# First block's attention: scores in pieces of at most 512 keys, one piece ahead, and reciprocal sums spread through memory

## The reference, cut to what matters

```python
for window, dilation in DILATED_PATTERNS:
    o_i, lse_i = dilated_window_attn(q, k, v, window, dilation)
    outs.append(o_i); lses.append(lse_i)
mix_w = jax.nn.softmax(jnp.stack(lses, axis=0), axis=0)
o = jnp.sum(mix_w[..., None] * jnp.stack(outs, axis=0), axis=0)
attn_out = o.reshape(B, S, ATTN_WIDTH) * jax.nn.silu(g_attn)
```

## Time and profile before

| | |
|---|---|
| time, median of 3 runs | 2654.49 us (2652.89 to 2657.09) |
| the profiled execution | 2656.93 us |
| its span in the trace | 2655.1 us |
| mean granted TensorE clock in it | 0.979 |
| TensorE busy over the span | 2502.4 us, 94% |
| VectorE, ScalarE, GpSimd busy | 1255.3, 1142.3, 596.3 us |

### The profile page before, as it was taken

One profiled execution on the slowest core, in us unless ns is written; L12 is line 12 of the kernel. 1 busy time (PEld: TensorE's weight loads), 2 busy tenths in 40 slices (PEclk: granted clock), 3 DMA queues, 4 the chain that ended last, 5 costly groups with the idle time before them and its releaser, 6 DMA issues. The chain is left out here.

```text
span 2655.1 us, 30070 instructions
## 1 busy us (share of the span) xinstructions
PE 2502.4 (94%) x11958; PEld 2004.0 (75%) x11958; DVE 1255.3 (47%) x1583; ACT 1142.3 (43%) x1612; POOL 596.3 (22%) x497
## 2 busy tenths in 40 slices
PE   8999998889999999999999999998978999999992
PEld 6888874448787888878887877885866888888882
DVE  6420315554303112126443943014138888888886
ACT  4212225553341222124232732244225777777773
POOL 1312302213131222233121741254101111111100
PEclk9999999999999999999999999999988999999996
DMA  4313121203310031233225633351546999999995
GB/s 174 107 64 92 54 82 40 80 13 132 111 64 32 32 130 46 72 108 105 90 68 203 238 135 111 103 183 45 177 174 242 376 380 377 388 381 373 374 363 232
DMA packets 146581, 434.78 MB, mean 164 GB/s; under 512 B 16232, under 2 KB 66632, under 8 KB 133768
## 3 DMA queue, kind: packets, MB, share of 16 engines
q1 hardware_dynamic: 95536, 374.23, 37.5%
q10 hardware_dynamic: 38120, 31.50, 3.6%
q0 software_dynamic: 12784, 27.11, 2.9%
HBM read 377.70 MB, written 72.91 MB: 170 GB/s over the span
## 5 line engine op out<-in xcount | busy, mean ns | idle before, releaser
L2795 DVE TENSOR_TENSOR ex_w_lo<-ex_w,ex_w_hi 128x2048 fp32r<-128x2048 f32 x198 | 448.0, 2290 | 73.3 <-ACT ex_w_hi L2734 71.4
L2734 ACT ACTIVATE ex_w_hi<-ex_w 128x2048 fp32r<-128x2048 f32 x198 | 378.9, 1915 | 21.6 <-PE ex_pb L2665 14.5
L220 POOL TENSOR_TENSOR p_w_lo<-w_raw,p_w_hi 128x512 fp32r<-128x512 f32 (+1 forms) x146 | 191.3, 1343 | 624.7 <-ACT p_w_hi L248 593.2
L220 POOL TENSOR_TENSOR p_w_lo_rest<-w_raw,p_w_hi_rest 128x512 fp32r<-128x512 f32 x88 | 118.0, 1373 | 255.9 <-ACT p_w_hi_rest L248 255.9
L845 DVE CUSTOM_DVE_ANT_0 att_sc<-att_ps_s,logc 128x128 f32<-128x128 f32 (+7 forms) x96 | 71.7, 752 | 120.8 <-PE att_ps_s L780 120.4
L273 PE MATMUL p_ps<-p_w_hi,hT_hi 128*128 128x512 f32 (+1 forms) x320 | 120.7, 377 | 0.0
L275 PE MATMUL p_ps<-p_w_hi,hT_lo 128*128 128x512 f32 (+1 forms) x320 | 118.3, 370 | 0.0
L274 PE MATMUL p_ps<-p_w_lo,hT_hi 128*128 128x512 f32 (+1 forms) x320 | 118.0, 369 | 0.0
L248 ACT ACTIVATE p_w_hi<-w_raw 128x512 fp32r<-128x512 f32 (+1 forms) x133 | 74.6, 599 | 91.2 <-PE mix_ps_rest L275 49.3
L2434 POOL DMA_INDIRECT ex_x<-xn_rows,slot_token x33 | 34.2, 1036 | 346.4 <-PE ex_px L2639 323.9
L273 PE MATMUL ex_py<-ex_w_hi,ex_hT_hi 128*128 128x512 f32 x264 | 107.3, 407 | 1.9 <-DVE ex_hT_lo L2804 1.9
(11 more groups left out here) (507 smaller groups left out, 6260.4 us busy)
## 6 DMA issues: line engine op xcount, KB each, us to landing
ex_w<-w SPq DMA_DIRECT2D x99, 2048.0 KB, 13.8
w_raw<-w_in SPq DMA_DIRECT2D x42, 1024.0 KB, 5.1
w_raw<-w_out SPq DMA_DIRECT2D x8, 1024.0 KB, 8.0
x_rows<-o_x SPq DMA_DIRECT2D x16, 512.0 KB, 2.6
qk_columns<-ml_qk_first ACTq DMA_DIRECT2D x16, 512.0 KB, 3.2
w_raw<-w_xkv SPq DMA_DIRECT2D x8, 1024.0 KB, 6.2
plain_cols<-x SPq DMA_DIRECT2D x8, 512.0 KB, 8.3
w_raw<-w_in SPq DMA_DIRECT2D x16, 256.0 KB, 3.9
```

The source lines that it names most:

```text
L220: emit(self.lo(n)[:, 0:w], self.half(n // (KC // 2), w)[:, n % (KC // 2), :], self.hi(n)[:, 0:w].bitcast(F32), ALU.subtract).then_inc(self ...
L2734: nc.scalar.activation(w_hi[:, n % RING, :], raw_half(n), ACT.Copy).then_inc(hi_done, 1)
L2795: nc.vector.tensor_tensor(w_lo[:, n % RING, :], raw_half(n), w_hi[:, n % RING, :].bitcast(F32), ALU.subtract).then_inc(down_lo if m == "w2 ...
```

## The change

**Pieces.** A row of more than 512 keys becomes two pieces, of 512 and of the rest: 12 pieces a pair. Each piece takes one bank of each head, alternating by its number. `scores` waits until the piece two before it has been taken out by both heads' `maxes`. For the second piece of a row, `maxes` starts from the first piece's result, a column in `nmx_first`, and not from a number.

**One piece ahead.** `items()` yields pieces for rows. TensorE issues piece 0 first and then, at the place of piece n, piece n+1. VectorE and ScalarE stay at the places of the pieces and rows. With two pieces ahead of one block, VectorE does the first piece's second head and the second piece's first head before the block's copy.

**Sums.** `spread_sums` and its matmuls, `keep_scales` and TensorE's wait on it are gone. SP waits for the reciprocals, stores the 1024 floats of a half to `sums_dram` with one DMA, waits for that, and loads them with two DMAs, each repeating 512 floats over 64 partitions, into `scales`. Queries, keys, V and weights are loaded from the same queue between these steps, in a new order. GpSimd's `scale` for a half now stands at the half's block 3, and `gate` after block 3 of the next half (block 2 before).

The diff, with the loads' and waits' lines:

```diff
-def attention(c, heads, q_dram, k_dram, v_dram, mixT, next_weights):
+def attention(c, heads, q_dram, k_dram, v_dram, sums_dram, mixT, next_weights):
...
+    def pieces(i):
+        hp, a = divmod(i, NT)
+        first = PER * hp + (a if a < HALF else 2 * a - HALF)
+        return range(first, first + (1 if a < HALF else 2))
+    row_of_piece = {m: (i, m - pieces(i)[0]) for i in range(PAIRS * NT) for m in pieces(i)}
     def items():
...
-            yield "rows", a
+            yield "piece", a
...
-                if hp == 0:
-                    yield "rows", HALF + j
-                elif j == 0:
-                    yield "rows", NT * hp + NT - 1
+                if hp == 0 or j == 0:
+                    for m in pieces(HALF + j if hp == 0 else NT * hp + NT - 1):
+                        yield "piece", m
...
-            yield "sums", 2 * hp
...
-                    yield "rows", NT * (hp + 1) + (j if j < HALF else j - 1)
+                    for m in pieces(NT * (hp + 1) + (j if j < HALF else j - 1)):
+                        yield "piece", m
...
-                if j == HALF - 1:
-                    yield "sums", 2 * hp + 1
...
+        nmx_first = s.enter_context(nc.sbuf_tensor("att_negmax_first", [P, PAIRS * 2 * NT], F32))
...
-        ps_s = s.enter_context(nc.psum_tensor("att_ps_s", [P, 2, S], F32))
+        ps_s = s.enter_context(nc.psum_tensor("att_ps_s", [P, 2, 2, BANK], F32))
...
-        inverted, spread, scales_kept, scaled = (c.sem(f"att_{n}") for n in ("inverted", "spread", "scales_kept", "scaled"))
+        inverted, sums_out, scaled = (c.sem(f"att_{n}") for n in ("inverted", "sums_out", "scaled"))
+        sums_in = [c.sem(f"att_sums_in{b}") for b in range(2)]
...
-        def bank_of(i, k):
-            a = i % NT
-            at = BANK * (a % 2) if a < HALF else 0
-            return ps_s[:, k, at:at + (a + 1) * P]
+        def columns_of_piece(m):
+            i, part = row_of_piece[m]
+            return slice(BANK * part, min(BANK * part + BANK, (i % NT + 1) * P))
...
         def sum_column(i, k):
...
-            return NT * (2 * hp + a // HALF) + 2 * (a % HALF) + k
+            return NT * (2 * hp + a // HALF) + HALF * k + a % HALF
...
         def columns(d):
...
             @block.sync
             def _(sp):
-                for hp in range(1, PAIRS):
-                    if hp >= 2:
-                        sp.wait_ge(scored, NT * (hp - 1))
-                    heads.load_qk(sp, hp, q_dram, k_dram)
-                    if hp >= 2:
-                        sp.wait_ge(summed, PER * (hp - 1))
-                    heads.load_v(sp, hp, v_dram)
-                    if hp == 1:
-                        next_weights.load(sp, 0, 2)
-                    if hp == 3:
-                        next_weights.load(sp, 2, 3)
-                    if hp == 4:
-                        next_weights.load(sp, 3, 4)
+                def spread_sums(d):
+                    sp.wait_ge(inverted, d + 1)
+                    with nc.allow_non_contiguous_dma(reason="8 sums a partition"):
+                        sp.dma_start(sums_dram[d].rearrange("(r p o) -> p r o", p=P, o=1),
+                                     rden[:, NT * d:NT * (d + 1)].unsqueeze(2)).then_inc(sums_out, 16)
+                    sp.wait_ge(sums_out, 16 * (d + 1))
+                    if d >= 2:
+                        sp.wait_ge(scaled, d - 1)
+                    for k in range(2):
+                        sp.dma_start(scales[HD * k:HD * (k + 1), d % 2, :], sums_dram[d, BANK * k:BANK * (k + 1)].partition_broadcast(HD)
+                                     ).then_inc(sums_in[d % 2], 16)
+                heads.load_qk(sp, 1, q_dram, k_dram)
+                heads.load_v(sp, 1, v_dram)
+                next_weights.load(sp, 0, 2)
+                for hp in range(PAIRS):
+                    if 1 <= hp < PAIRS - 1:
+                        sp.wait_ge(scored, PER * hp)
+                        heads.load_qk(sp, hp + 1, q_dram, k_dram)
+                    spread_sums(2 * hp)
+                    if 1 <= hp < PAIRS - 1:
+                        sp.wait_ge(summed, PER * hp)
+                        heads.load_v(sp, hp + 1, v_dram)
+                    spread_sums(2 * hp + 1)
+                    if hp in (2, 3):
+                        next_weights.load(sp, hp, hp + 1)
...
             @block.gpsimd
             def _(pool):
                 def scale(d):
-                    pool.wait_ge(scales_kept, d + 1)
+                    pool.wait_ge(sums_in[d % 2], 32 * (d // 2 + 1))
...
-                    if kind == "sums":
-                        scale(n)
+                    if kind == "block" and block_at(n)[2] == 3:
+                        scale(2 * (n // PER) + block_at(n)[1])
...
             @block.tensor
             def _(pe):
-                def scores(i):
+                def scores(m):
+                    i, part = row_of_piece[m]
...
-                    if i >= 1:
-                        pe.wait_ge(maxed, 2 * i if a == 0 or a >= HALF else 2 * (i - 1))
-                    for u in range(0, (a + 1) * P, BANK):
-                        for k in range(2):
-                            at, end = slice(HD * k, HD * k + HD), min(u + BANK, (a + 1) * P)
-                            ins = pe.matmul(bank_of(i, k)[:, u:end], qk[hp % 2][at, 0, a * P:(a + 1) * P],
-                                            qk[hp % 2][at, 1, u:end], start=True, stop=True)
+                    if m >= 2:
+                        pe.wait_ge(maxed, 2 * (m - 1))
+                    to = columns_of_piece(m)
+                    for k in range(2):
+                        at = slice(HD * k, HD * k + HD)
+                        ins = pe.matmul(ps_s[:, k, m % 2, 0:to.stop - to.start], qk[hp % 2][at, 0, a * P:(a + 1) * P],
+                                        qk[hp % 2][at, 1, to], start=True, stop=True)
...
                 def turn(n, k):
...
-                def spread_sums(d):
-                    pe.wait_ge(inverted, d + 1)
-                    if d >= 1:
-                        pe.wait_ge(gated, d)
-                    for r in range(HALF):
-                        for k in range(2):
-                            at = NT * d + 2 * r + k
-                            ins = pe.matmul(ps_o[HD * k:HD * (k + 1), 1 - d % 2, r * P:(r + 1) * P],
-                                            rden[:, at:at + 1].to_broadcast([P, HD]), c.const("ident"),
-                                            start=True, stop=True)
-                    ins.then_inc(spread, 1)
                 def values(n):
...
-                    if j == 0 and n >= 1:
-                        pe.wait_ge(scales_kept, 2 * hp + half)
-                        if n > HALF:
-                            pe.wait_ge(gated, 2 * hp + half - 1)
+                    if j == 0 and hp >= 1:
+                        pe.wait_ge(gated, 2 * hp + half - 1)
...
+                scores(0)
...
-                    if kind == "rows":
-                        scores(n)
-                    elif kind == "sums":
-                        spread_sums(n)
+                    if kind == "piece":
+                        if n + 1 < len(row_of_piece):
+                            scores(n + 1)
...
             def _(dve):
...
-                def maxes(i, k):
+                def maxes(m, k):
+                    i, part = row_of_piece[m]
...
-                    dve.wait_ge(scored, i + 1)
+                    at, to = 2 * i + k, columns_of_piece(m)
+                    dve.wait_ge(scored, m + 1)
...
-                    nc.vector.tensor_tensor_reduce(row_of(i, k), bank_of(i, k), logc[:, S - (a + 1) * P:S], -SCALE, -NEG,
-                                                   ALU.add, ALU.min, nmx[:, 2 * i + k:2 * i + k + 1]).then_inc(maxed, 1)
+                    largest = nmx if m == pieces(i)[-1] else nmx_first
+                    so_far = nmx_first[:, at:at + 1] if part else -NEG
+                    if part:
+                        dve.wait_ge(maxed, 2 * m + k - 1)
+                    table = slice(S - (a + 1) * P + to.start, S - (a + 1) * P + to.stop)
+                    nc.vector.tensor_tensor_reduce(row_of(i, k)[:, to], ps_s[:, k, m % 2, 0:to.stop - to.start],
+                                                   logc[:, table], -SCALE, so_far, ALU.add, ALU.min,
+                                                   largest[:, at:at + 1]).then_inc(maxed, 1)
...
                 def invert(d):
...
-                    if kind == "rows":
+                    if kind == "piece":
...
-                        if late is not None and late < rows_before(n):
+                        if late is not None and row_of_piece[late][0] < rows_before(n):
...
-                        if j == 2 and n > 2:
+                        if j == HALF - 1 and n >= HALF:
...
             def _(act):
                 def exps(i):
...
-                        act.wait_ge(maxed, 2 * i + k + 1)
+                        act.wait_ge(maxed, 2 * pieces(i)[-1] + k + 1)
```

(18 more changed lines are left out.)

## The result

The changed kernel takes 2667.55 us in the median, against 2654.49 before. One of its five executions took 9897.54 us for a reason that no run explains; the median of the other four is 2667.2, and the ratio goes by them: 1.0044, with a 95% interval of 1.0032 to 1.0057. The profiled execution took 2666.88 us with a span of 2665.1, 10.0 more than before. So it lasts 218.7 us in place of 209.7: the stage holds 9.0 of the 10.0.

A forecast was written before the change was run, and what follows sets the result against it. TensorE was taken to set the pace, with waits in its holes. Terms 1.3 + 4 x 0.55 + 1.0 + 0.9 = 5.4 us off 2654.5 gave 2649.1; own range 2643 to 2655, 8 in 10 from 2637 to 2660.

The forecast's parts named there:

- the late memory path: Slower rival: store and loads exceed 14.7 us, gates hold VectorE's copies back, 10 us in all at the upper bound: 2659; chance 0.13.
- Sums through memory: Reciprocals' store and two loads: bounds 7.1 to 16.7 us, taken as 5.2 + 3 = 8.2.
- The queue: SP's order behind a store: next queries and keys go out near block 6, first asked for 19 us later.
- The loads: Two 128 KB loads repeating the reciprocals over 64 partitions: taken as 3 us of the 8.2 us path.
- The cover: Time from a first half's reciprocals to the gate, less GpSimd's work: 14.7 us steady, 9.9 in the last pair.
- The walk of the order: One steady pair on TensorE: five new waits for maxima, together 4.13 us; period 34.00 becomes 33.45, 0.55 us gained.
- The fast rival: Scores never wait for the second head's maximum: period 29.3 us, time 2628; chance 0.17.
- The second piece's bound from a column: VectorE's maxima of second pieces: no extra cost, or 0.08 us each, thrice a pair, 1.2 us in all.
- The sums: Twelve groups of 16 reciprocal matmuls leave TensorE: 0.87 us each, 1.74 a pair.
- The last pair: Period into the last pair, without scores of a next one: 32.57 us, 1.01 less than before.
- The first pair: Stage start to block 4's transposes: walked as 20.9 us against 23.4 before; 1.3 gained with low clock, 2.5 without.
- the dip: Low granted clock (0.72 before) on TensorE in the first pair, expected again, costing 1.2 us.

The follow-up runs named there:

- the turned store: Changed kernel, with VectorE transposing the reciprocals in 32x32 squares so a store writes 32 pieces of 128 bytes in four DMAs: 2651.53 us.
- Keys before the odd store: Changed kernel, with SP loading the next pair's queries and keys ahead of the second half's store: 2661.60 us.
- without the store: Changed kernel with the reciprocals' store and its wait left out, 512 floats of another input loaded instead (wrong numbers): stage 204.4 us, one execution of 2651.40.
- whole rows: Kernel before, its rows not cut into pieces, with the sums through memory and the store as 32 pieces of 128 bytes: 2647.57 us.
- pieces and maxima first: Changed kernel with VectorE's second-head maximum ahead of the next block's copy: 2650.27 us with sums on TensorE, 2641.55 through memory with 128-byte store pieces.
- the maxima first: Changed kernel with the store in 128-byte pieces, and VectorE doing the second head's maximum ahead of the next block's copy: 2641.55 us.

## Why the prediction was wrong

It forecast 2649 us, faster or the same; the kernel is slower, and the rival that came true is the late memory path, at 0.13, by more than the 10 us that it was given.

**The step that failed is the term "Sums through memory".** It priced the store at 5.2 us, after a load of 2048 single floats, and set aside the 11.0 us of a load of 1024 because larger loads were queued ahead of it. The store measured 9.9 us in the median, 8.4 to 12.0, and 8.4 us with nothing large ahead of it (575.56). The price lay by the upper bound and not by the lower one. The Trainium skill's rule that was quoted there (DMA: Bandwidth & Descriptors, Rules for kernel authors: one descriptor per element, rearrange) pointed to this side; the turned store, 2.2 us and a ninth of the small packets, agrees with it.

**Three links behind the price were not walked, or walked wrongly.**
- The queue. The step let the keys go out near block 6. There, at 448.03, 6.7 us after block 4's transposes, SP issued only the odd store, since it had served the even half first; the keys followed at 458.96, 17.6 after block 4, and at 528.68, 19.3 after it, with the weights ahead. That left 6.7 us before they were asked for in place of 19. Price: 0.7 + 3.35 us, and 1.2 of low clock. "Keys before the odd store" shows it.
- The loads. They took 5.6 to 5.8 us and not 3 for most first halves, and 10.9 where the next store followed them by 1.1 us. In the last pair store and loads came to 19.3 us (575.56 to 594.85) against a cover of 9.9: the excess of 9.4 is the gate's wait of 9.54. The cover was right and the path more than twice the 8.2 us that it was priced at, and above the upper bound of 16.7.
- The clock. No step charged a stall for what follows it. It was 1.2 us behind the keys and 1.4 behind the gate.

Together: 4.07 + 1.2 + 7.9 (9.37 less 1.44 at block 9) + 1.4 = 14.6 us, against 14.3 between the stages with and without the store. The rival had 2.0 us of lateness a pair for the steady gates; they did not wait at all (the only such wait in the stage is the 9.54), as 14.1 us from store to multiplication (504.18 to 518.24; 13.9 to 14.3 in the pairs before the last) just fits in 14.7. It had nothing for the keys.

**What held.** *The walk of the order:* 33.61 against 33.45 a pair; waits of 0.55, 0.82, 1.14, 0.70 and 0.31 idle against 0.63, 0.89, 1.38, 0.69 and 0.54, in the five places named; from start to start no step of the pair is off by more than 0.13. The fast rival without these waits did not come. *The second piece's bound from a column:* 746 ns against 683 for the plain 512, so 0.06 us each, within the 0 to 0.08. *The sums:* 1.74 to 1.76 us a pair in three comparisons (35.37 less 33.61, 33.34 less 31.59, 34.00 less 32.26), walked as 1.74. *The last pair:* 32.66 against 32.57. *The first pair:* 21.09 us against 20.9 without the dip; I had expected the dip and 22.1, because the walk had TensorE no busier there. It is busier, 13.31 us and not 10.99 between 385 and 402, and the dip is absent. That term was 1.0 us too small, and makes up for the 0.16 by which each of four periods is longer; that the stage without a store comes to 204.4 against 204.3 is in part this luck.

**Where the change stands without the store's fault.** The four versions with a cheap memory path or none divide its gain. Sums off TensorE gain 8.7 us by time at whole rows (2656.25 less 2647.57) and 8.7 with pieces and maxima first. The pieces in their order, one ahead and with the second maximum behind the copy, lose 4 (2651.53 less 2647.57). With the maxima first they gain 6 (2647.57 less 2641.55). So the pieces are worth something only together with VectorE's order, which the change left as it was. The rule by which the fast rival went (the Trainium skill: Perfetto Trace Analysis, Optimizing Scalar/DVE Operations) says only that breaking instructions up may let work end sooner. As the change stands it did not: with the copy ahead of the maximum that TensorE waited for, the pieces lost 4 us; with the maximum ahead they gained 6.

**Open.** By what means a store of single floats holds loads that were issued before it, and why 1.1 us behind them it does and 1.8 us behind, with the load of V between, it hardly does. The turned store changed the size of the pieces, the partitions that they come from and the number of DMAs at once; no run parts them. And the execution of 9897.54 us.

## What to carry to other kernels

Price a transfer by the size of its contiguous pieces and not by its bytes: where the trace has two prices for the nearest kind, and the low one only with an excuse for the high one, take the high one and see what it stalls. On an engine or queue that works in order, walk everything behind a blocking wait to its last user, and the last pass of a loop by itself, where the cover is thinnest. When work is cut into smaller pieces so that others wait less, check that the piece waited for also comes earlier in its engine's order; here that order was worth 10 us with the pieces and nothing without them.

## What the runs showed of the hardware

- 1024 single floats from SBUF to memory took 8.4 to 12.0 us; the same 4 KB as 32 pieces of 128 bytes in four DMAs took 2.2 to 2.8 us.
- From issue to use, two loads of 128 KB took 10.9 to 11.5 us where such a store was issued 1.1 us behind them (three kernels); 5.15 with the store held until they had landed; 5.6 to 5.8 (kernel after) with a load of 512 KB and then a store 1.8 us or more behind; 3.4 to 4.1 between turned stores.
- After a stretch in which TensorE was busy 1.15 of 4.5 us, the next 4 us had a granted clock of 0.57. The dip of the first pair was there in three of four profiles with whole rows, after 17 us from the stage's start in which TensorE was busy 11.4 to 11.5 us (12.8 in the fourth), and in none of nine with pieces, where it was busy 13.1 to 14.0.
- VectorE's maximum over 128x512 took 746 ns with its bound from a column and 683 ns with it from a number.
